# The modulation product on four column groups of the array, with VectorE adding the four partial rows

## What is computed

```python
for l in range(DEPTH):                                     # DEPTH = 2
    mod   = silu(c)     @ w_mod[l] + b_mod[l]              # w_mod[l]: (1024, 6144)
    mod_c = silu(c_ctx) @ w_mod[l] + b_mod[l]
    sh1, sc1, g1, sh2, sc2, g2 = split(mod, 6)
    h  = rmsnorm(x, norm1[l]) * (1 + sc1) + sh1            # the same for ctx with mod_c
    ... one input projection, three attention branches, gated merge, output projection
    x = x + g1 * merged
    h2 = rmsnorm(x, norm2[l]) * (1 + sc2) + sh2
    x = x + g2 * top2_of_16_experts(h2)                    # context tokens too in layer 0
return rmsnorm(x, final_norm)
```

## Time and profile before

| | |
|---|---|
| median of 3 runs | 2110.77 us (2109.45 to 2118.57) |
| profiled execution, first to last instruction | 2108.4 us |
| PE busy | 2012.3 us, 95% of the span |
| DVE / ACT / POOL busy | 495.8 / 368.3 / 123.5 us |
| DMA | 388.43 MB, mean 184 GB/s |
| modulation products, PE busy | 170.0 us in 384 instructions |

### The profile page before, as it was taken

The page is one execution under the profiler, slowest core; times in us unless marked ns, Lnnn a source line. Parts: engine busy times, 40 slices in busy tenths (PEclk is TensorE's granted clock), DMA queues, the critical chain, the costliest instruction groups (busy, mean ns, idle before and its releaser), DMA issues. The chain is left out here.

```text
span 2108.4 us, 16774 instructions
## 1 busy us (share of the span) xinstructions
PE 2012.3 (95%) x6259; PEld 943.3 (45%) x6259; DVE 495.8 (24%) x1256; ACT 368.3 (17%) x797; POOL 123.5 (6%) x186
## 2 busy tenths in 40 slices
PE   7999999999999999999999999999999969999992
PEld 1244445564444444344444424445644434444441
DVE  0332035651011134101010155125501220101002
ACT  1011035551000110010010012125500110101001
POOL 1100000010000000100000020000200000000001
PEclk9999999999999998999999999999999969999996
DMA  9932210011113036999999794220143279999962
GB/s 333 381 140 80 80 51 1 6 26 60 69 51 120 18 133 247 326 342 327 344 327 339 261 336 169 80 90 1 36 141 113 81 272 350 324 340 340 327 216 90
DMA packets 178038, 388.43 MB, mean 184 GB/s; under 512 B 22834, under 2 KB 26962, under 8 KB 177964
## 3 DMA queue, kind: packets, MB, share of 16 engines
q1 hardware_dynamic: 142784, 322.97, 43.1%
q0 software_dynamic: 17056, 58.00, 7.2%
q10 hardware_dynamic: 18132, 6.58, 1.2%
HBM read 366.45 MB, written 21.07 MB: 184 GB/s over the span
## 5 line engine op out<-in xcount | busy, mean ns | idle before, releaser
L1464 PE MATMUL bank<-ring_sb,QR_sb 128*128 128x512 f32 x1024 | 447.6, 595 | 3.5 <-ACT QR_sb L765 3.5
L1464 PEld LDWEIGHTS bank<-ring_sb,QR_sb 128*128 128x128 f32 x1024 | 193.3, 191 | 235.3 <-issue 230.7
L1309 PE MATMUL bank<-ring_sb,HT_sb 128*128 128x512 f32 x672 | 295.9, 596 | 2.7 <-ACT HT_sb L614 1.5
L1375 PE MATMUL bank<-ring_sb,HT_sb 128*128 128x512 f32 x576 | 253.3, 593 | 1.4 <-ACT QR_sb L731 1.4
L1475 PE MATMUL bank<-ring_sb,QR_sb 128*128 128x512 f32 x512 | 225.2, 593 | 1.7 <-issue 1.7
L1309 PEld LDWEIGHTS bank<-ring_sb,HT_sb 128*128 128x128 f32 x672 | 126.0, 191 | 149.4 <-issue 147.4
L1375 PEld LDWEIGHTS bank<-ring_sb,HT_sb 128*128 128x128 f32 x576 | 109.5, 190 | 138.5 <-issue 136.6
L1260 PE MATMUL bank<-ring_sb,cT_sb 128*2 128x512 f32 x384 | 170.0, 603 | 1.4 <-DMA ring_sb<-w_mod 1.4
L1475 PEld LDWEIGHTS bank<-ring_sb,QR_sb 128*128 128x128 f32 x512 | 95.1, 190 | 110.0 <-issue 110.0
L1337 PE MATMUL bank<-KR_sb,QR_sb 64*128 64x512 f32 (+1 forms) x288 | 141.4, 575 | 1.6 <-ACT QR_sb L649 1.6
L1364 PE MATMUL bank<-WK_sb,KR_sb 128*64 128x128 f32 x960 | 136.9, 283 | 0.0
(11 more groups left out here) (177 smaller groups left out, 1192.0 us busy)
## 6 DMA issues: line engine op xcount, KB each, us to landing
ring_sb<-w_e_gate SPq DMA_DIRECT2D x32, 2048.0 KB, 9.5
ring_sb<-w_e_up SPq DMA_DIRECT2D x32, 2048.0 KB, 8.8
ring_sb<-w_e_down SPq DMA_DIRECT2D x32, 2048.0 KB, 10.0
ring_sb<-w_mod SPq DMA_DIRECT2D x24, 2048.0 KB, 12.0
ring_sb<-w_in SPq DMA_DIRECT2D x22, 2048.0 KB, 13.7
y_d<-KR_sb POOLq DMA_DIRECT2D x32, 512.0 KB, 8.5
ring_sb<-w_branch SPq DMA_DIRECT2D x6, 2048.0 KB, 7.6
MB_sb<-mod_d POOLq DMA_DIRECT2D x16, 512.0 KB, 8.0
```

The costliest lines, as they stand in the source:

```text
L1309: ins = mm(bank[j % 4][:, :], HT[:, k, P * t:P * t + P], WR[slot][:, k], start=(k == 0), stop=(k == KD - 1))
L1375: ins = mm(bank[i % 2][:, :], HT[:, k, P * t:P * t + P], WR[wg][:, k], start=(k == 0), stop=(k == KD - 1))
L1464: ins = mm(bank[j][:, :], hgT[parity][:, c8], WR[s][:, c8], start=(c8 == 0), stop=(c8 == KD - 1))
```

## The change

The eight blocks of a modulation product go in turn to four groups of 32 array columns: block k writes partitions 32 (k mod 4) and the next one of the bank. Each of the four places gets a sum over two blocks. VectorE adds the bias to the first of the four and then the other three to it, in linked steps, before the scale step where there is one. Loads, banks, waits and the order of the work stay as they are.

```diff
+MOD_COLS = 4
@@ mod_rows (VectorE)
-                row, b, made = mrow[i % n], bmod[i], bank[MOD_BANK[i]][0:2, :]
+                row, b = mrow[i % n], bmod[i]
                 part, half = divmod(j, 2)
-                if part in (1, 4):
-                    link(tt(row, made, b, ALU.add))
-                    stt(row, row, 1.0, nrow[l][part // 4][:, CW * half:CW * half + CW], ALU.add, ALU.mult)\
-                        .then_inc(mod_row, 1)
-                else:
-                    tt(row, made, b, ALU.add).then_inc(mod_row, 1)
+                scaled = part in (1, 4)
+                link(tt(row, bank[MOD_BANK[i]][0:2, :], b, ALU.add))
+                for c in range(1, MOD_COLS):
+                    ins = tt(row, bank[MOD_BANK[i]][32 * c:32 * c + 2, :], row, ALU.add)
+                    if scaled or c < MOD_COLS - 1:
+                        link(ins)
+                if scaled:
+                    ins = stt(row, row, 1.0, nrow[l][part // 4][:, CW * half:CW * half + CW], ALU.add, ALU.mult)
+                ins.then_inc(mod_row, 1)
@@ modulation (TensorE)
                 for k in range(KD):
-                    ins = mm(bank[use][0:2, :], cT[:, k, :], WR[slot][:, k], start=(k == 0), stop=(k == KD - 1))
+                    c = 32 * (k % MOD_COLS)
+                    ins = mm(bank[use][c:c + 2, :], cT[:, k, :], WR[slot][:, k], start=(k < MOD_COLS),
+                             stop=(k >= KD - MOD_COLS))
                 ins.then_inc(mod_mm, 1)
```

## The result

The changed kernel takes 2094.91 us (median of 4 runs, 2091.62 to 2098.69) where the kernel before takes 2110.55 (4 runs beside them, 2109.45 to 2118.57): a ratio of 0.9917, with a 95% interval of 0.9891 to 0.9942. That is 15.6 us won by the medians. It lies inside the range on record (2079 to 2115) and 6.9 us above the forecast of 2088. The profiled execution took 2094.57 us, its span is 2092.9 us, 15.5 less than before, where the forecast's sum was 23.

A forecast was written before the change was run, and what follows sets the result against it. PE, busy 95% of the span, was taken to bound the kernel. Terms of -12.5, -14 and +3.5 gave -23 us: span 2085.4, plus 2.4 to the median, 2088 us; 8-in-10 range 2079 to 2115.

The forecast's parts named there:

- the forecast's sum: Whole kernel: -12.5 at the start, -14 at the router, +3.5 at the end of layer 0, -23 us.
- the three places: Where modulation products run: the start (12 products), behind the router (8), the end of layer 0 (4).
- The pace of the product: Each modulation product: two instructions run at a time, 3.9 us in place of 6.87 us.
- The 1.3 us a product of bare weight loads: Each product: by the skill's rule, 16 weight loads of 0.08 us would stand bare; the trace disagreed for same columns.
- The start: First twelve products: weights' DMA becomes the limit, projection starts at 89.5 in place of 102.08, 12.5 us won.
- The router: Eight products behind the router: VectorE's rows, then the gather, are late next; experts 15.3 us earlier, 14 taken.
- The 1.3 us that the sum took off for the low clock: Router: after idling, PE's three products might end 3.5 us later, gain 13.7 in place of 15.3; 14 taken.
- The rival of four at a time and a cold array: Products at 1.7 us, idle PE's clock falls, first expert and projection pay up to 3.5 us each; 2092 us, chance 0.10.
- The end of layer 0: Last four products: PE waits for VectorE's added steps, third projection tile 2.7 us later; 3.5 us lost taken.
- No overlap: All products: the array takes one matmul at a time, only the end of layer 0 loses 3; 2114 us, chance 0.14.
- drain: All products: each change of column group costs about 0.09 us and nothing overlaps; 2128 us, chance 0.09.
- Partial overlap: All products: some overlap, 5.4 us each; 11 won at start, 9 at router, 3.5 lost; 2094 us, chance 0.07.

The follow-up runs named there:

- VectorE's steps alone: Kernel before, one column group, plus three linked VectorE steps a row that leave the row as it is: 2118.48 us, ratio 1.0024.
- the third place alone: Changed kernel with four column groups only in the last four products, one group in the first twenty: 2115.23 us, ratio 1.0015.
- 4, 4 and 1 groups: Changed kernel with four column groups in the first twenty products and one in the last four: 2090.83 us, ratio 0.9900.
- 2, 2 and 1: Changed kernel with two column groups in the first twenty products and one in the last four: 2080.09 us, ratio 0.9840.

## Why the prediction was right or wrong

The way, the three places and what is late at each were right; 15.5 us came of the 23 by the spans. The pace that the sum was built on was wrong by a factor of two, and the sum did not need it. What fell short is the low clock, in a term of the router and in one that the sum did not have.

**The pace of the product: wrong, and without effect.** The step said that the second pass of a block holds up the instruction behind it, so that two run at a time and a product takes 3.9 us. It is four at a time and 1.90 us, and the order in the program makes no difference (1.92 us). The statement beside it, that any pace up to some 4.3 us gives nearly the same sum, held: the projection starts at 89.50 with 1.90 us and at 90.00 with 3.60, and with every product done twice the ratio to the kernel before is 0.9911, against 0.9923 with the products done once. Two groups are better at the router for VectorE's sake, not for their pace.
The estimate of 2.9 us from the 2.38x that the Trainium skill measured for three groups ("TensorE: Matmul & The Clock Gate", Part 3, Measured speedup vs the span model) was nearer than mine. The 1.3 us a product of bare weight loads that the text worked out from the same part have no room in 1.90 us: the loads lie beside the matmuls. The Trainium skill ("TensorE: Matmul & The Clock Gate", Part 3, The mechanism) also lets a load go ahead of running matmuls into a background weight buffer; the text left that out, and the loads seen beside matmuls on the same rows agree with it.

**The start: right.** 89.5 was forecast and 89.50 measured, by the reason given: eight blocks of 2 MB at 387 GB/s behind block 5. That sum ends at 88.5, and the microsecond on top was a choice.

**The router: right in VectorE's steps, short by 2.8 us.** Less the 12.9 us of lead, the forecast's times were: row 2 delayed by a store until 811.0 (measured 811.25, with 2.63 us of wait for that store), the one-hots done at 824.4 (824.70), the row numbers at 831.1 (831.07), the gather's issue at 832.9 (832.66), the experts at 842.1 (844.00). The last step lacked the clock on the transposes and their copy (3.12 us from 840.88 to 844.00, 2.27 before) and about a microsecond of the gather. So 13.4 us in place of 15.3 by the experts' start. PE's own times were wrong with the pace: it was to be idle some 6 us for the one-hots and 2 for the gather, and was 14.09 and 6.60. The 1.3 us that the sum took off for the low clock stood at the wrong work: they were to fall on the three products ahead of the gather, which in fact ended 6.6 us before it landed, and 2.2 us fell on the first expert. The rival of four at a time and a cold array has this cold first expert as it was written, and its 2092 was closer than the forecast; it had no term for the attention stages either, so part of that is luck.

**The end of layer 0: the number right, by another way.** 2.7 us lost where the text worked out 2.7 and took 3.5. The text had PE wait for the last tile of `h`, late by the steps of rows 9, 10 and 11. That tile was ready where it said, but PE came to it no sooner: the first transposes were 1.5 us late (2.1 in the text for row 9's steps, and so they took, but the gather landed 0.7 sooner), and 1.2 came from the second tile and the low clock. That both ways give 2.7 is luck. The run of VectorE's steps alone shows that VectorE is the reason in the main: 3.5 us lost there with no change on PE at all, 2.6 of them by the later start of the transposes.

**The missing term: the clock in stages that the change does not touch.** The sum assumed that what is won at one place stays won to the end. From layer 1's projection to the end 5.9 us went, 4.8 of them in the first 23 us of its attention, where almost nothing but the clock differed (0.79 in place of 0.91 over 40 us). With these 5.9 and the 2.8 us that the router fell short, less 0.8 at the end of layer 0 and 0.4 in small steps, the 23 us of the sum are 15.5. The forecast looked at the clock only behind stretches that the change makes idle, and took the low stretches of the trace before (7 us in the attention) as fixed. They are not: with nothing changed ahead of it, the run of the third place alone had 0.91 in place of 0.97 over 100 us of layer 0's attention. What brings the loss stays open. The four profiles with four groups everywhere lost 5.1 to 7.4 us in the two attentions, but 4, 4 and 1 groups lost 5.2, and 2, 2 and 1 lost 4.6. PE's idle time in the places is not shown to lead to it: the third place alone idled 25.19 us and lost 0.3 in the attention behind it, 4, 4 and 1 groups idled 2.12 us there and lost 2.7, and each product done twice took much of the idle time away and lost 5.1 in both attentions.

**The rivals.** No overlap and drain are out with the first burst of four. Partial overlap is out too. The bursts follow at 0.43 us, without a gap where the group changes; with this the Trainium skill's statement that only a change of the tiling mode drains the array ("TensorEngine Tiling (Array Packing)", Key Properties) agrees.

**What a better forecast would have asked:** not how fast the product gets, but how much of that speed the three places can take. The start needs less than 5.4 us a product, and two groups give 3.60. The router pays 0.71 us for each further step of VectorE on the five rows that stand ahead of the gather. At the end PE waits for VectorE anyway, so further steps can only cost. These waits were to be read from the rows of before, the pace of two groups was not. They lead to two groups at the first 20 products and one at the last four: 2080.09 us.

## What to carry to other kernels

Before splitting an accumulation over column groups, find out how fast it has to be at each place, and take the fewest groups that reach it: here two gave 28 us and four gave 15.5 in the same batch, in the main because each further group adds a linked step of 0.71 us on VectorE to rows that others wait for. Where PE is not what comes last, leave the work on PE alone. And when a change turns PE's work into waiting, price the low clock on what follows, and give the total a margin for it (1.6 us for each 0.001 of mean clock in the kernel before), for it also moves in stages that the change does not touch.

## What the runs showed of the hardware

- Four fp32 matmuls on four groups of 32 columns run at once: bursts of four, 0.43 us apart; a product by itself takes 1.90 us against 7.03, four one behind the other 7.05 against 27.63, a factor of 3.9. Two groups: 3.60 and 13.90 us, a factor of 2.0. The order in the program did not matter (1.92 us).
- The weight loads of the other groups cost nothing that can be seen: in the burst at 72.69 eight loads and four matmuls lie in the same 40 ns, and at 73.11 four loads beside four matmuls that begin and four that began 0.43 us sooner.
- The clock fell to its low level in the start, where PE had a product of 1.90 us (3.59 at the low level) in a beat of 5.4 us (0.50 from 35 to 40 us). With two groups, 3.6 us in the same beat, it was 1.00 in that stretch and 0.50 from 60 to 65 us, where PE had been waiting.
- The time of the unchanged kernel follows its mean granted clock, 2107.3 us at 0.977 to 2118.9 at 0.970, and with the same program a stage of 100 us was seen at 0.97 and at 0.91.
- A linked VectorE step on a 2x512 row that reads PSUM costs 0.71 us in a chain (three in 2.13), the same as one on SBUF (three in 2.10 in the run of VectorE's steps alone).
